# State-space parameters made step by step inside the input projection, and the next quarter's rows placed ahead of the output transposes

## The reference, cut to what matters

```python
x = _rmsnorm(h, norm1_g)
proj = x @ w_in.astype(f32)
u = proj[..., :D_SSM]
zr = proj[..., D_SSM:]
...
dt = jnp.exp(log_dt)[:, None]
mag = jnp.exp(lam_re * dt)
ab_re = mag * jnp.cos(lam_im * dt)
ab_im = mag * jnp.sin(lam_im * dt)
den = lam_re * lam_re + lam_im * lam_im
nr = ab_re - 1.0
f_re = (nr * lam_re + ab_im * lam_im) / den
f_im = (ab_im * lam_re - nr * lam_im) / den
bb_re = f_re[..., None] * b_re - f_im[..., None] * b_im
bb_im = f_re[..., None] * b_im + f_im[..., None] * b_re
bu_re = jnp.einsum('blgc,gpc->blgp', ug, bb_re)
bu_im = jnp.einsum('blgc,gpc->blgp', ug, bb_im)
...
_, _, h_re, h_im = lax.associative_scan(combine, (a_re, a_im, bu_re, bu_im), axis=1)
y = jnp.einsum('blgp,gcp->blgc', h_re, c_re) - jnp.einsum('blgp,gcp->blgc', h_im, c_im)
y = y.reshape(bsz, seq_len, D_SSM) + d_skip * u
y = jax.nn.gelu(y)
y = y * jax.nn.sigmoid(y @ w_glu + b_glu)
```

## Time and profile before

| | |
|---|---|
| median of 3 runs | 3567.74 us (3566.04 to 3571.64) |
| the profiled execution | 3568.36 us, its span 3566.6 us |
| TensorE busy | 3250.8 us, 91% |
| VectorE busy | 2132.0 us, 60% |
| ScalarE busy | 1190.6 us, 33% |
| GpSimd busy | 231.6 us, 6% |
| mean granted TensorE clock | 0.952 |

### The profile page before, as it was taken

One profiled execution on the slowest core, in us unless ns is written; L12 is line 12 of the kernel. 1 busy time (PEld: TensorE's weight loads), 2 busy tenths in 40 slices (PEclk: granted clock), 3 DMA queues, 4 the chain that ended last, 5 costly groups with the idle time before them and its releaser, 6 DMA issues.

```text
span 3566.6 us, 75773 instructions
## 1 busy us (share of the span) xinstructions
PE 3250.8 (91%) x32916; PEld 3097.8 (87%) x32916; DVE 2132.0 (60%) x4032; ACT 1190.6 (33%) x2339; POOL 231.6 (6%) x225
## 2 busy tenths in 40 slices
PE   6899945879999989878899999999999999999997
PEld 6899944648788877878899999999999999999997
DVE  6654569426777777433565555655555655555555
ACT  4332323424544545323332222322222322223432
POOL 0000033000111111002100000000000000000111
PEclk9999977889999999879999999999999999999998
DMA  4444310010010000033322222222222222222222
GB/s 151 129 128 135 117 49 14 3 38 24 25 33 24 24 24 19 16 91 100 100 69 68 66 67 69 66 72 66 72 71 66 71 71 72 66 68 75 72 89 88
DMA packets 332587, 237.72 MB, mean 67 GB/s; under 512 B 16720, under 2 KB 319440, under 8 KB 332240
## 3 DMA queue, kind: packets, MB, share of 16 engines
q1 hardware_dynamic: 332256, 232.87, 22.3%
HBM read 206.28 MB, written 25.38 MB: 65 GB/s over the span
## 4 chain that ended last, share of the span: by engine, by line
PE 49%; DVE 3%; DMA 2%; issue 1%; ACT 1%; SPq 0%; DVEq 0%; ACTq 0%
PE tail_bank L987 28%; PE tail_bank L1024 13%; PE tail_bank L1043 5%; PE tail_bank L975 2%; DMA tail_raw<-in_w_out 2%; PE tail_bank L1056 1%; ACT tail_w_hi L634 1%; DVE tail_x L787 0%; DVE tail_xn_lo L792 0%; DVE tail_xn_lo L775 0%; DVE mix_b L799 0%; DMA tail_raw<-in_w_pg 0%; DVE mix_b L918 0%; DMA tail_raw<-in_w_gate 0%; DVE mix_a L893 0%
## 5 line engine op out<-in xcount | busy, mean ns | idle before, releaser
L987 PE MATMUL tail_bank<-tail_xn_hi,tail_w_hi 128*128 128x352 f32 x2112 | 682.5, 323 | 9.1 <-DVE tail_xn_lo L792 9.1
L987 PE MATMUL tail_bank<-tail_xn_lo,tail_w_hi 128*128 128x352 f32 x2112 | 680.3, 322 | 0.0
L987 PE MATMUL tail_bank<-tail_xn_hi,tail_w_lo 128*128 128x352 f32 x2112 | 680.3, 322 | 0.0
L987 PEld LDWEIGHTS tail_bank<-tail_xn_hi,tail_w_hi 128*128 128x128 f32 x2112 | 397.5, 188 | 12.9 <-issue 6.9
L987 PEld LDWEIGHTS tail_bank<-tail_xn_lo,tail_w_hi 128*128 128x128 f32 x2112 | 397.7, 188 | 0.1
L987 PEld LDWEIGHTS tail_bank<-tail_xn_hi,tail_w_lo 128*128 128x128 f32 x2112 | 397.6, 188 | 0.0
L1024 PE MATMUL tail_bank<-tail_f_hi,tail_wd_hi 128*128 128x352 f32 x1056 | 341.7, 324 | 7.0 <-DVE mix_b L893 2.7
L1024 PE MATMUL tail_bank<-tail_f_lo,tail_wd_hi 128*128 128x352 f32 x1056 | 339.6, 322 | 0.0
L1024 PE MATMUL tail_bank<-tail_f_hi,tail_wd_lo 128*128 128x352 f32 x1056 | 339.6, 322 | 0.0
L634 ACT CAST tail_w_hi<-tail_raw 128x1024 fp32r<-128x1024 f32 x180 | 185.4, 1046 | 401.9 <-DMA tail_raw<-in_w_gate 205.4
L770 DVE TENSOR_TENSOR tail_w_lo<-tail_raw,tail_w_hi 128x1024 fp32r<-128x1024 f32 x180 | 220.6, 1226 | 159.6 <-ACT tail_w_hi L634 159.2
(11 more groups left out here) (447 smaller groups left out, 6692.4 us busy)
## 6 DMA issues: line engine op xcount, KB each, us to landing
tail_raw<-in_w_gate SPq DMA_DIRECT2D x66, 512.0 KB, 4.0
tail_raw<-in_w_val SPq DMA_DIRECT2D x66, 512.0 KB, 4.0
tail_raw<-in_w_down SPq DMA_DIRECT2D x66, 512.0 KB, 3.6
in_raw<-in_w_in SPq DMA_DIRECT2D x54, 512.0 KB, 4.1
in_xs<-in_xT SPq DMA_DIRECT2D x12, 1408.0 KB, 6.8
scratch_zr<-in_zo SPq DMA_DIRECT2D x84, 176.0 KB, 1.9
rw_z<-scratch_zr SPq DMA_DIRECT2D x16, 896.0 KB, 5.6
tail_raw<-in_w_out SPq DMA_DIRECT2D x24, 512.0 KB, 4.5
```

The source lines that it names most:

```text
L987: mm = pe.matmul(out[:, 0:TW], l, r, start=(k == 0 and j == 0), stop=(k == KD - 1 and j == 2))
```

## The change

The parameter buffers move to an object `Poles` that outlives both stages. Its eight inputs are loaded at the start of the projection, behind the first loads of SP's queue. The parameter chain is cut into 23 steps: "angles", "phase", "phases" (three), "rho", "hold", "B", "powers" (three), "R" (six) and "CA" (six). VectorE does one step in one weight block of the `zr` passes, from the third such block on, right after `weights_lo`; the first block of a pass and its last two have none. ScalarE does the three activations of the chain at two of these blocks.

In the state space the `Ks` products come first, ahead of `own_rows(0)`. `R` has a buffer that is ready at the start, and `turn_high` is still written over it. The doublings of `turn_low` are done by VectorE. `Ks` lies in the buffer `T`, so VectorE waits for the transfers to `Tm` before `rotate(0)`. In each quarter all three `outputs` come first, then `own_rows` and `driven` of the quarter after next, then all `channels`, on TensorE and on ScalarE.

The diff, cut to its core (the bodies of the parameter steps are the lines that are removed further down, sorted under names):

```diff
+class Poles:
...
+    LOADS = 8
...
+def pole_parameters(dve, poles):
...
+    def step(name, part=0):
+        if name == "angles":
+            dve.wait_ge(poles.par_in, 16 * poles.LOADS)
+            dve.wait_ge(poles.dt_ready, 1)
+            tt(s["th"], li[:], dt[:], ALU.mult)
+            dve.tensor_tensor(s["mag"], lr[:], dt[:], ALU.mult).then_inc(poles.mag_ready, 1)
+            reduced(s["rs"], s["th"])
+            ts(s["x1"], s["rs"], math.pi / 2, None, ALU.add)
+            reduced(s["rc"], s["x1"])
+            dve.sem_inc(poles.arg_ready, 1)
+        elif name == "phase":
+            dve.wait_ge(poles.sc_ready, 3)
+            squared(pw[1], [s["cos"], s["sin"]])
+            squared(pw[2], pw[1])
+            squared(pw[0], pw[2])
+            unit(pw[0], s["rho"])
+        elif name == "phases":
+            for i in ((1, 2, 3), (4, 5, 6), (7,))[part]:
+                squared(pw[i], pw[i - 1])
+                if i % 3 == 0:
+                    unit(pw[i])
...
+        elif name == "R":
+            product(R, powers(L), [x[:].unsqueeze(2).to_broadcast([P, NJ, L, GC]) for x in Bb], big[:, :, 0:L, :], part)
...
-def project_in(nc, ins, outs, scratch, u):
+def project_in(nc, ins, outs, scratch, u, poles):
...
+        first_z = TH * KU
+        POLES = [("angles", 0), ("phase", 0), ("phases", 0), ("phases", 1), ("phases", 2), ("rho", 0), ("hold", 0), ("B", 0)]
+        POLES += [("powers", i) for i in range(3)] + [(name, i) for name in ("R", "CA") for i in range(6)]
+        FREE = [b for b in range(first_z + 2, NB_) if BLOCKS[b][2] not in (KU, KIN - 2, KIN - 1)]
+        POLES_AT = dict(zip(FREE, POLES))
...
+                for to, name in poles.loads():
+                    sp.dma_start(to, ins[name]).then_inc(poles.par_in, 16)
...
+                        if i == NS * first_z:
+                            act.wait_ge(poles.par_in, 16 * poles.LOADS)
+                            act.activation(poles.dt[:], poles.dt[:], ACT.Exp).then_inc(poles.dt_ready, 1)
+                        if i == NS * (FREE[0] + 1):
+                            mag, s_ = poles.small["mag"], poles.small
+                            act.wait_ge(poles.mag_ready, 1)
+                            act.activation(mag[:], mag[:], ACT.Exp).then_inc(poles.sc_ready, 1)
+                            act.wait_ge(poles.arg_ready, 1)
+                            act.activation(s_["sin"][:], s_["rs"][:], ACT.Sin).then_inc(poles.sc_ready, 1)
+                            act.activation(s_["cos"][:], s_["rc"][:], ACT.Sin).then_inc(poles.sc_ready, 1)
...
                             weights_lo(b)
+                        if i // NS in POLES_AT:
+                            pole_step(*POLES_AT[i // NS])
                         for n in range(NS):
...
+        turn_low, turn_high = e.sb("turn_low", [P, 2, NJ, HALF_NB]), poles.R
...
+        Ks = T[0:GC].rearrange("p k j n -> p (k j n)").rearrange("p (g x) -> p g x", x=P)
...
+                dve.wait_ge(zero, 5)
+                w = 1
+                for i in range(NW - 1):
+                    by = [bcast(x[:, i, :], w) for x in Pw]
+                    first, then = [[turn_low[:, x, :, a:a + w] for x in range(2)] for a in (0, w)]
+                    cmul(then, first, by, spare[:, 0:NJ * w].rearrange("p (j n) -> p j n", n=w))
+                    w *= 2
                 dve.wait_ge(r_mm, NR)
...
+                dve.wait_ge(t_moved, 16 * L)
...
                 for ct in range(KU):
                     pe.wait_ge(h_ready, ct + 1)
-                    outputs(ct, 0)
-                    outputs(ct, 1)
-                    channels(ct, 0)
-                    outputs(ct, 2)
-                    channels(ct, 1)
-                    channels(ct, 2)
+                    if ct == 0:
+                        pe.wait_ge(par_in, 16 * NPAR)
+                    for lot in range(NLOT):
+                        outputs(ct, lot)
                     if ct + 2 < KU:
                         own_rows(ct + 2)
                         driven(ct + 2)
+                    for lot in range(NLOT):
+                        channels(ct, lot)
```

More of the change, by code:

```diff
@@ L58, in tok, with __init__, loads @@
     return slice(n * TW, (n + 1) * TW)
-def project_in(nc, ins, outs, scratch, u):
+NG_ = 32
+GC = 16
+NS = 64
+L = P // GC
+NJ = NG_ // 2
+NBL = SEQ // L
+NBS = DB
+NBT = NBL + NBS
+HALF_NB = NBL // 2
+JC = NJ // KU
+GB_ = NG_ // KU
+TWO_PI = 2 * math.pi
+PI_A = 6.28125
+PI_B = TWO_PI - PI_A
+ROUND = 1.5 * 2 ** 23
+BELOW_PI = 3.1415925
+NW = 8
+class Poles:
+    def __init__(self, e):
+        self.lr, self.li, self.dt = (e.sb(n, [P, NJ]) for n in ("lr", "li", "dt"))
+        self.B = e.sb("B", [P, 2, NJ, GC])
+        self.C = [e.sb(n, [P, NJ, GC]) for n in ("Cr", "Ci")]
+        self.ident = e.sb("ident", [P, P])
+        self.small = {n: e.sb(n, [P, NJ]) for n in ("th", "mag", "k", "rs", "rc", "sin", "cos", "den", "nr", "fr", "fi", "x1", "x2", "rho")}
+        self.Ap = [e.sb(n, [P, L + 1, NJ]) for n in ("Apr", "Api")]
+        self.Pw = [e.sb(n, [P, NW, NJ]) for n in ("Pwr", "Pwi")]
+        self.Bb = [e.sb(n, [P, NJ, GC]) for n in ("Bbr", "Bbi")]
+        self.CA = [e.sb(n, [P, NJ, L + 1, GC]) for n in ("CAr", "CAn")]
+        self.R = e.sb("R", [P, 2, NJ, P])
+        self.big = e.sb("big", [P, NJ * (L + 1) * GC])
+        self.par_in, self.chain = e.sem("par_in"), e.sem("chain")
+        self.dt_ready, self.mag_ready, self.sc_ready, self.arg_ready = e.sem("dt_ready"), e.sem("mag_ready"), e.sem("sc_ready"), e.sem("arg_ready")
+        self.ones_put = e.sem("ones_put")
+    LOADS = 8
+    def loads(self):
+        return ((self.lr[:], "lam_re"), (self.li[:], "lam_im"), (self.dt[:], "log_dt"), (self.ident[:], "ident"), (self.B[:, 0], "b_re"),
+                (self.B[:, 1], "b_im"), (self.C[0][:], "c_re"), (self.C[1][:], "c_im"))
@@ L1955, in u_turn @@
         def u_turn(ct, lot, f):
[L1957 removed]
+            return ct * UT + lot * 4 + f + max(ct - 2, 0) * XT
         def x_turn(ct, lot, half):
[L1961 removed]
+            return min(ct + 3, KU) * UT + ct * XT + lot * 2 + half
         def upto(ct):
@@ L2078, in channels @@
                         act.copy(dst, bk_t[i % 2][:, 0:4 * n].rearrange("p (t n) -> p t n", t=4)).then_inc(t_out, 1)
+                for c in range(KU):
+                    for q in range(2):
+                        i = 2 * c + q
+                        act.wait_ge(k_mm, i + 1)
+                        act.copy(Ks[:, GB_ * c + q:GB_ * (c + 1):2, :], bk_y[i % 4][0:GC, :].rearrange("p (g x) -> p g x", x=P)).then_inc(k_out, 1)
                 own_rows(0)
@@ L2134, in cmul @@
                     tt(out[1], out[1], t, ALU.add)
-                s = {n: x[:] for n, x in small.items()}
-                def reduced(out, x):
-                    ts(s["k"], x, 1 / TWO_PI, ROUND, ALU.mult, ALU.add)
-                    ts(s["k"], s["k"], -ROUND, None, ALU.add)
-                    link(dve.scalar_tensor_tensor(out, s["k"], -PI_A, x, ALU.mult, ALU.add))
-                    link(dve.scalar_tensor_tensor(out, s["k"], -PI_B, out, ALU.mult, ALU.add))
-                    ts(out, out, BELOW_PI, -BELOW_PI, ALU.min, ALU.max)
@@ L2350, in channels @@
                         last.then_inc(t_mm, 1)
-                own_rows(0)
-                pe.wait_ge(r_ready, 1)
-                for i in range(NR):
-                    if i >= 4:
-                        pe.wait_ge(r_out, i - 3)
-                    x, j0 = i // (NJ // 4), 4 * (i % (NJ // 4))
-                    for j in range(j0, j0 + 4):
-                        last = pe.transpose(bk_y[i % 4][:, (j - j0) * P:(j - j0 + 1) * P], R[x][:, j].rearrange("p s c -> p (s c)"), ident[:])
-                    last.then_inc(r_mm, 1)
-                pe.wait_ge(r_out, NR)
-                driven(0)
-                pe.wait_ge(ca_ready, 1)
                 for c in range(KU):
@@ L2375, in _ @@
                         last[q].then_inc(k_mm, 1)
+                own_rows(0)
+                pe.wait_ge(k_out, 2 * KU)
+                for i in range(NR):
+                    if i >= 4:
+                        pe.wait_ge(r_out, i - 3)
+                    x, j0 = i // (NJ // 4), 4 * (i % (NJ // 4))
+                    for j in range(j0, j0 + 4):
+                        last = pe.transpose(bk_y[i % 4][:, (j - j0) * P:(j - j0 + 1) * P], R[x][:, j], ident[:])
+                    last.then_inc(r_mm, 1)
+                pe.wait_ge(r_out, NR)
+                driven(0)
                 own_rows(1)
                 driven(1)
-                pe.wait_ge(k_out, 2 * KU)
                 pe.wait_ge(t_moved, 16 * L)
```

289 lines of the change are left out of this document (118 added, 171 removed).

## The result

Median of four executions: 3567.14 us before, 3508.18 us after; ratio 0.9834, 95% interval 0.9817 to 0.9851. The same kernel was timed once more among the experiments, on another occasion: 3501.02 against 3566.6, ratio 0.9820 (0.9807 to 0.9834). The forecast, 3506, is a ratio of 0.9829 to the 3567.14, between the two, and both intervals hold it. The profiled execution took 3510.45 us (span 3508.7), against 3568.36.

What follows compares the result with a forecast made beforehand. The state-space stage was taken as bound by VectorE's parameter chain, then a ring in which rotate(2) waited for ScalarE's eviction of driven(2). 3568.36 - 61.8 = 3506.6, less 0.62 to the median: 3506, range 3497 to 3519.

Steps and rivals of the forecast that it cites:

- The parameters: State-space opening: with the shorter VectorE parameter chain, outputs(0) starts at 542.4 instead of 601.00, 58.6 us earlier.
- Contention: Doublings of turn_low on VectorE: GpSimd's two operations beside them cost nothing to 2 us; 1 taken.
- The new order: State space from outputs(0) at 542.4 to the gate at 645.2, including 1.6 us for lots at 1.2 GHz.
- no slow clock: State space: TensorE keeps its clock behind the new piece, 1.6 us less, 3504; chance 0.18.
- slow in all three `outputs`: State space: the clock falls in all three outputs and both own_rows, 3513; chance 0.10.
- the order gives nothing: State space: channels merely moves, only the parameters' 58.6 us stay, 3509; chance 0.07.
- The projection: Weight blocks given the 23 steps: lateness grows to 3.5 us, inside 4.4, then drains; 0 us lost.
- a ring of 4.69: Projection: scaled_out, own_share, weights_hi, weights_lo (3.54) and the other tile (1.15); steps over 2.95 us make weights_lo late.
- slack: Projection: TensorE wants the low half of the weights only 4.4 us after it was done.
- The eight loads: Projection start, SP's queue: third weight block's issue moves from 12.80 to about 16.5, covered by 17 us.
- dear steps: Projection: R and CA cost as much as beside a busy GpSimd, TensorE waits 9 us, 3515; chance 0.10.
- not faster: Projection: no slack, each step's length falls on TensorE in full, about 56 us plus slow clock, 3577; chance 0.05.

Runs made afterwards that it cites:

- e1_old_order: The changed kernel with the old order of outputs, channels, own_rows and driven on TensorE and ScalarE; 3512.27 us, ratio 0.9842 to the kernel before.
- e6_again: The changed kernel timed and profiled once more, unaltered; 3501.02 us against 3566.6, ratio 0.9820.
- e2_order_only: The kernel before with only the new order of outputs, own_rows, driven and channels; 3564.0 us, ratio 0.9986.
- e5_longer_steps: The changed kernel with one more VectorE operation of 2048 to 2304 columns in each of the 23 steps; 3545.93 us, ratio 0.9938.

## Why the prediction was right, step by step

- **The parameters (58.6).** Right. The first `outputs` came 544.42 - 482.27 = 62.15 us after GpSimd began to clear `Tm`, where 61.4 was forecast (57.8 us gained for 58.6), and `e1_old_order` gives 56 us for this half alone. Contention was set at 1 us and measured (0.96 - 0.19) + (1.47 - 0.42) = 1.8. `Tm` and the transposes of `R` (501.19 to about 505) were in time: neither `turn_high` nor `rotate(0)` waited.
- **The new order (102.8 from the first `outputs` to the gate).** The mechanism was right and the size off, twice. At full clock the sum was 101.2 and the chip took 97.4: most pieces were rounded up by 0.3 to 0.8 (`own_rows` and `driven` 14.2 instead of 14.8, third lots 3.7, the last two `channels` 5.4 and 5.3 instead of 6.1; the first two took the 5 forecast). And the clock, set at 1.6, cost from nothing (97.41) to 7.9 (105.32) in the same program. A caught lot was priced at 1.8 from the 5.74 of the first one before, but only its beginning was at 1.2 GHz, as these windows of the kernel before show (busy, granted clock); the caught lots took 5.30 to 6.85, up to 2.9 over 3.96.

```profile
601.00:604.00 3.00, 3.00 (x14) 0.50 0.00 0
...
605.00:607.00 2.00, 2.00 (x34) 1.00 0.00 0
```

So the rival "no slow clock" described `e6_again`, and something close to "slow in all three `outputs`" described the first profile, though `own_rows(2)` kept its clock there. The rival "the order gives nothing" is refuted by `e2_order_only`. `rotate(3)` ended 3.7 us ahead of `outputs(3)` in the first profile and 0.8 in `e6_again` (2.4 forecast): at full clock VectorE nearly sets the pace.
- **The Trainium skill's rule** ("TensorE: Matmul & The Clock Gate", "What's actually happening"), that the slow clock follows an idle array: `e6_again` agrees (1.00 at 572 to 580), the first profile does not (0.50 at 578 to 582, with TensorE never idle over 1.2 us from 544 on).
- **The gate.** Not foreseen: it took 57.07 instead of 58.76 us, with a granted clock of 1.00 at its start. It goes with the order: 57.07 in `e2_order_only`, 58.77 in `e1_old_order`.
- **The projection.** Right, and now shown: a ring of 4.69 and the step (9.32 and 6.99 us a block), with 4.4 us of slack. In the changed kernel the lateness grew by 1.6, 0.8 and 0.8, to 3.2 (3.5 forecast), and drained; TensorE was busy 321.67 us. The eight loads cost nothing: the third weight load left at 15.06 instead of 12.80, and TensorE's start was no later. The rival "dear steps" is real in its price and absent for its condition: GpSimd does nothing there. The rival "not faster" (no slack) is refuted: 3.2 us of lateness cost TensorE nothing, and in `e5_longer_steps`, where the lateness outgrew the slack, some 55 us of added operations made the passes 37.1 longer.
- **The sum.** 60.2 us gained within the stage, less 1.3 by which it opens later and 1.0 behind it: 57.9 = 3568.36 - 3510.45, where 61.8 was forecast. The 1.3 is no more than two profiles of one kernel differ by: GpSimd's first fill of the stage came at 480.83 before and 482.11 after, but at 482.10 in the kernel before again and 480.90 in the changed kernel again. The second pair of profiles, 3568.97 and 3501.23, lies 67.7 apart. That 3506 came within 2.2 us of the median 3508.18 is thus in part luck: pieces rounded up, a gate that was shorter and a clock that cost more offset each other.
